# Next-to-last feed-forward chunk: two low parts of GpSimd behind VectorE's low part of B21, and the low part of B11 moved ahead of two sums

## The chip, the cores and the metric

The kernel runs on one core of one Trainium2 chip. The metric is the device time of one execution in microseconds, taken as a median over runs; the profile is one further execution with its own time.

## The reference

Two layers over a sequence of 1024 tokens with 1024 features, float32. Layer 0 mixes tokens by a gated spatial MLP, layer 1 by chunked band attention; each is followed by the same feed-forward block, which is where the change lies:

```
def swiglu(h, w_gate, w_up, w_down):
    return (jax.nn.silu(h @ w_gate) * (h @ w_up)) @ w_down

hn = rms_norm(x, norm_ffn_g[i])
x = x + swiglu(hn, ffn_w_gate[i], ffn_w_up[i], ffn_w_down[i])      # D_FF = 2816
```

## The kernel before

**Arithmetic.** Each float32 operand is split into a high part (fp32r) and a low part (the difference), and each product is three matmuls: high by high, low by high, high by low (L934 to L936). In the middle of each feed-forward block the matrix products are done in a seven-product form of a 2 by 2 blocked product. The seven left operands (weights) are called A11, A12, S2, S3, S1, A22 and S4; their right partners in the down projection are B11, B21, T2, T3, T1, T4 and B22. B parts are quarters of the hidden tensor (`h_full`, high `h_hi`, low `h_lo`, the low part written over the full one), T parts are sums of them (`t_full`, `t_hi`, `t_lo`).

**Tiling and stages.** The hidden size is cut into 11 chunks of 256. Each chunk does seven gate products, seven up products, and the seven down products of the chunk before. Chunks 2 to 8 are a loop. The next-to-last chunk ("late", number 9, `LATE`) does its own down products too, right behind its up products, with names `down_products(it, True)`; the last chunk (number 10) is written out by hand with all its gate and up products interleaved, in the order of `PROD_LAST`, and a plain down projection at its end. There are two feed-forward blocks, F1 and F2, with the same code.

**Who does what.** TensorE runs the products in a fixed order, each behind waits on semaphores: `made` (GpSimd's parts of the weights), `t_lo` (VectorE's low parts of the right side), `d_added` (VectorE's additions out of the PSUM banks). For the down products it waits in front of product number pos for `t_lo` at pos + 1, and from pos 2 on for the additions of product pos - 2 (L1103 to L1117). ScalarE makes high parts: `left_high` (L1600) of the weights, `right_high` (L1589) of the right side, in late in the order B11, B22, T1, T3, T2, then the weights at places 5 and 6, then B21 and T4. VectorE forms the hidden parts, the sums T1, T3, T2 (`first_sums`, L2084 to L2087) and T4 (`last_sum`, L2092), the low parts (`right_low`, L2078) and the additions to x (`down_adds`, L2103). GpSimd makes, group by group, the sums of weight blocks and their low parts (`middle_group`; `low` is L716, `high` is L713); the four raw weight blocks b[0] to b[3] are `raw_block`.

**Queues.** SP loads the next weight block into a `raw_block` as soon as GpSimd has finished the last low part that reads it: buffer 0 behind "lo S2", 2 behind "lo S3", 3 behind "lo A22", 1 behind "lo S4" (`gate_up`, DMA at L584). Behind the late down group, GpSimd works on the last chunk: `group` is called twice, and there it makes high parts too. It starts with the high parts of A11 (buffer 0) and A12 (buffer 1; waits for that load and for the late down product A12), then "sum S1" (L793; waits for the loads of buffers 2 and 3), then without a rest down to "lo A22". The second group is the same with the loads that the first released, except that its A12 waits for the last chunk's gate product A12; behind it come high and low parts of the last down weights (`d_hi`, `d_lo`). TensorE's down projection waits for the last of these, "lo d1".

Of the kernel before, what the change touches and what calls it, by code (L numbers as in the profile page):

```python
# [99 lines left out]
LATE = CHUNKS - 2  # L100

AT_G0, AT_D, AT_G1, AT_D_LATE = -5, -4, -3, -2
# [4 lines left out]
def middle(it, at, per, i):  # L107

    return it * (3 * per) + (at * per + i)
# [44 lines left out]
def trunk(nc, x_t, gains, v_gain, w_s_t, b_s, rel_rev, ident_d, w_units, f_blocks, f_down, out_t):  # L154
# [4 lines left out]
    with ExitStack() as ctx:  # L159
# [196 lines left out]
        def r32(ap):  # L356
            return ap.bitcast(F32)
# [84 lines left out]
        def hidden_part(t, f, h):  # L442
            return t[:, f, toks(h)]
# [4 lines left out]
        def right_full(name):  # L448
            return t_full[name][:, :] if name in t_full else hidden_part(h_full, *H_PART[name])

        def right_hi_of(name):
            return t_hi[name][:, :] if name in t_hi else hidden_part(h_hi, *H_PART[name])

        def right_lo_of(name):
            return t_lo[name][:, :] if name in t_lo else hidden_part(h_lo, *H_PART[name])
# [218 lines left out]
        def _(pool):  # L674
# [40 lines left out]
            def low(out, full, hi, made):  # L715
                pool.tensor_tensor(out, full, r32(hi), ALU.subtract).then_inc(made, 1)  # L716

            def ffn(name):
                s = hid[name]
# [21 lines left out]
                def middle_group(it, at):  # L741


                    def loaded(i):
                        pool.wait_ge(s.block_in[i], middle(it, at, 16, 16 * 4))

                    def after(op):
                        pool.wait_ge(s.made, middle(it, at, MID, MID_MADE + (MIDDLE[op] if op else 0)))

                    def low_part(op, b_, before):  # L750
                        slot = ORDER.index(op)
                        pool.wait_ge(s.left_hi, middle(it, at, 7, 7 + slot + 1))
                        after(before)
                        low(lo[slot], b_, hi[slot], s.made)

                    loaded(2)
                    loaded(3)
                    after(None)
                    pool.tensor_tensor(s1_sum[:, :], b[2], b[3], ALU.add).then_inc(s.made, 1)  # L759
                    low_part("A11", b[0], "sum S1")  # L760
                    after("lo A11")
                    pool.tensor_tensor(b[2], b[0], b[2], ALU.subtract).then_inc(s.made, 1)
                    low_part("A12", b[1], "sum S3")
                    after("lo A12")
                    pool.tensor_tensor(b[0], s1_sum[:, :], b[0], ALU.subtract).then_inc(s.made, 1)
                    after("sum S2")
                    pool.tensor_tensor(b[1], b[1], b[0], ALU.subtract).then_inc(s.made, 1)
                    low_part("S2", b[0], "sum S4")
                    low_part("S3", b[2], "lo S2")
                    low_part("S1", s1_sum[:, :], "lo S3")  # L770
                    low_part("A22", b[3], "lo S1")
                    low_part("S4", b[1], "lo A22")

# [1122 lines left out]
        def _(dve):  # L1896
# [165 lines left out]
            def ffn(name, n):  # L2062
# [9 lines left out]
                def right_low(it, name, sums=0):  # L2072

                    order = HI_LATE if isinstance(it, int) and it == LATE else HI_ORDER
                    dve.wait_ge(w.t_hi, it * 7 - 7 + (order.index(name) + 1))
                    if sums:
                        dve.wait_ge(w.t_full, it * 4 - 4 + sums)
                    dve.tensor_tensor(right_lo_of(name), right_full(name), r32(right_hi_of(name)), ALU.subtract  # L2078
                                      ).then_inc(w.t_lo, 1)

                def first_sums(it):
                    b11, b12, b22 = (hidden_part(h_full, f, h) for f, h in ((0, 0), (0, 1), (1, 1)))
                    dve.wait_ge(w.full, it * 4 + (3 if isinstance(it, int) and it == LATE else 4))
                    dve.tensor_tensor(right_full("T1"), b12, b11, ALU.subtract).then_inc(w.t_full, 1)  # L2084
                    dve.tensor_tensor(right_full("T3"), b22, b12, ALU.subtract).then_inc(w.t_full, 1)
                    dve.wait_ge(w.t_full, it * 4 - 4 + 1)
                    dve.tensor_tensor(right_full("T2"), b22, right_full("T1"), ALU.subtract).then_inc(w.t_full, 1)  # L2087
# [218 lines left out]
                def one(it, kind):  # L2306
                    if kind == "first":
                        first_chunk()
                        return
                    if kind == "last":  # L2310
                        last_chunk(it)
                        return

                    def product(g, op):
                        dve.wait_ge(w.prod, N_PROD.at(it, len(PROD) * g + PROD[op]))

                    def snap(i):
                        dve.wait_ge(w.snap, N_SNAP.at(it, i))

                    def added(i, act):  # L2320
                        dve.wait_ge(w.cadd, N_CADD.at(it, i))
                        dve.wait_ge(w.act, it * 4 + act)

                    up_order = ORDER[:5] + ["S4", "A22"] if kind == "late" else ORDER

                    def up_product(op):
                        dve.wait_ge(w.prod, N_PROD.at(it, len(PROD) + up_order.index(op) + 1))

                    if kind != "second":
                        first_sums(it - 1)  # L2330
                        last_sum(it - 1)
                        right_low(it - 1, "B11", 1)
                    if kind != "second":
                        product(0, "A12")
                        snap(1)
                        cadd(gated[0][:, :], bank[1])
                        right_low(it - 1, "B21", 4)
                        right_low(it - 1, "T2", 4)
                        right_low(it - 1, "T3")
                    product(0, "S1")  # L2340
                    snap(3)
                    cadd(gated[2][:, :], bank[0])
                    product(0, "A22")
                    cadd(gated[1][:, :], bank[1])
                    if kind != "second":
                        right_low(it - 1, "T1", 3)
                        right_low(it - 1, "T4")
                        right_low(it - 1, "B22", 3)
                        for pos in range(7):
                            down_adds(it, False, pos)  # L2350
                    up_product("A12")
                    snap(4)
                    cadd(hidden_part(h_full, 0, 0), bank[3])
                    added(4, 1)
                    times(gated[0][:, :], 0, 0)
                    up_product("S1")
                    snap(6)
                    cadd(hidden_part(h_full, 1, 1), bank[2])
                    added(5, 2)
                    times(gated[2][:, :], 1, 1)  # L2360

                    def last_01():
                        up_product("S4")
                        dve.wait_ge(w.act, it * 4 + 4)
                        dve.tensor_tensor(hidden_part(h_full, 0, 1), bank[2][:, :], gated[3][:, :], ALU.mult).then_inc(w.full, 1)

                    def last_10():
                        up_product("A22")
                        cadd(hidden_part(h_full, 1, 0), bank[3])
                        added(6, 3)  # L2370
                        times(gated[1][:, :], 1, 0)

                    if kind != "late":
                        last_10()
                        last_01()
                        return
                    last_01()
                    first_sums(it)
                    right_low(it, "B11", 1)
                    last_10()  # L2380
                    last_sum(it)
                    right_low(it, "B21", 4)
                    right_low(it, "T2", 4)
                    down_adds(it, True, 0)
                    right_low(it, "T3")
                    right_low(it, "T1", 3)
                    down_adds(it, True, 1)
                    right_low(it, "T4")
                    right_low(it, "B22", 3)
                    for pos in range(2, 7):  # L2390
                        down_adds(it, True, pos)
# [240 lines left out]
```

## Time and profile before

| what | value |
|---|---|
| median of 3 runs | 2569.73 us (2568.29 to 2572.27) |
| time of the profiled execution | 2570.11 us |
| its span | 2568.0 us, so 2.1 us lie around it |
| TensorE busy | 2448.7 us, 95% of the span |
| VectorE, ScalarE, GpSimd busy | 1679.1, 1010.8, 1286.7 us |
| mean granted clock of TensorE | 0.991 |

TensorE works nearly all the time, so a change counts by the idle time of TensorE that it adds or removes. GpSimd is busy for half of the span on average, but in the last chunk of a feed-forward block for most of the time.

### The profile page before, as it was taken

What the parts mean: (1) busy time and instruction counts of PE and PEld (TensorE: products, weight loads), DVE (VectorE), ACT (ScalarE), POOL (GpSimd) and SP (SyncE); (2) the same over time, 40 slices, a digit from 0 to 9 for tenths busy, and PEclk for the clock granted to TensorE, in tenths of its full rate; (3) what the DMA queues carried; (4) which work ended last, traced back from release to release, by engine and by line L of the source; (5) the groups of instructions that cost most, each with busy time, mean ns of one, the idle gap of its engine ahead of it and who ended that gap; (6) DMA issues with size and microseconds to landing.
All of it is one profiled execution on the core that took longest, in us unless ns stands there. A gap on an engine that the chain in (4) does not pass through costs nothing. (4 is left out here: it accounts for less than half of the span.)

```text
span 2568.0 us, 36361 instructions
## 1 busy us (share of the span) xinstructions
PE 2448.7 (95%) x11464; PEld 2019.0 (79%) x11464; DVE 1679.1 (65%) x2667; ACT 1010.8 (39%) x1831; POOL 1286.7 (50%) x898
## 2 busy tenths in 40 slices
PE   8998999999999999998989999999989999999987
PEld 7886888887788888886777777777767888888876
DVE  6246665667476777665866666676676677677755
ACT  5112211124434333331465555566544334433323
POOL 5242223213788888777312112221135878878776
PEclk9998999999999999999999999999999999999998
DMA  4232122111111211111111011111011111121111
GB/s 173 88 113 78 67 78 67 59 35 46 46 58 49 61 53 57 57 50 50 60 36 33 19 42 43 43 37 41 9 45 37 53 58 53 50 64 50 58 58 66
DMA packets 70522, 143.74 MB, mean 56 GB/s; under 512 B 7312, under 2 KB 17696, under 8 KB 69936
## 3 DMA queue, kind: packets, MB, share of 16 engines
q1 hardware_dynamic: 52912, 119.72, 14.7%
q10 hardware_dynamic: 17536, 23.07, 2.6%
q8 instruction: 42, 0.69, 0.1%
q14 instruction: 32, 0.26, 0.0%
HBM read 130.13 MB, written 12.63 MB: 56 GB/s over the span
## 5 line engine op out<-in xcount | busy, mean ns | idle before, releaser
L716 POOL TENSOR_TENSOR a_lo<-raw_block,a_hi 128x512 fp32r<-128x512 f32 x364 | 508.9, 1398 | 158.4 <-ACT a_hi L1600 134.2
L678 POOL TENSOR_SCALAR w_hi<-raw 128x1024 fp32r<-128x1024 f32 x80 | 90.7, 1133 | 830.7 <-PE bank L936 587.5
L1600 ACT ACTIVATE a_hi<-raw_block 128x512 fp32r<-128x512 f32 x324 | 202.4, 629 | 330.8 <-PE bank L936 122.4
L934 PE MATMUL bank<-T_hi,a_hi 128*128 128x512 f32 x672 | 262.6, 391 | 3.5 <-issue 3.0
L936 PE MATMUL bank<-T_hi,a_lo 128*128 128x512 f32 x672 | 261.7, 389 | 0.0
L935 PE MATMUL bank<-T_lo,a_hi 128*128 128x512 f32 x672 | 261.5, 389 | 0.0
L934 PE MATMUL bank<-B_hi,a_hi 128*128 128x512 f32 x576 | 224.9, 390 | 2.6 <-DVE h_full L2067 1.7
L936 PE MATMUL bank<-B_hi,a_lo 128*128 128x512 f32 x576 | 224.2, 389 | 0.0
L935 PE MATMUL bank<-B_lo,a_hi 128*128 128x512 f32 x576 | 224.1, 389 | 0.0
L680 POOL TENSOR_TENSOR w_lo<-raw,w_hi 128x1024 fp32r<-128x1024 f32 x80 | 198.8, 2485 | 6.7
L2067 DVE TENSOR_TENSOR h_full<-bank,h_full 128x512 f32<-128x512 f32 x54 | 37.3, 691 | 211.6 <-PE bank L936 198.2
L934 PEld LDWEIGHTS bank<-T_hi,a_hi 128*128 128x128 f32 x672 | 126.1, 188 | 33.9 <-issue 7.0
L936 PEld LDWEIGHTS bank<-T_hi,a_lo 128*128 128x128 f32 x672 | 126.1, 188 | 26.4
L935 PEld LDWEIGHTS bank<-T_lo,a_hi 128*128 128x128 f32 x672 | 126.2, 188 | 25.7
L934 PE MATMUL bank<-T_hi,w_hi 128*128 128x512 f32 x320 | 131.3, 410 | 15.6 <-issue 9.6
L2103 DVE TENSOR_TENSOR x<-bank,x 128x512 f32<-128x512 f32 x216 | 142.3, 685 | 0.0
L759 POOL TENSOR_TENSOR s_sum<-raw_block,raw_block 128x512 f32<-128x512 f32 x54 | 78.5, 1454 | 117.4 <-PE bank L936 87.6
L934 PE MATMUL bank<-B_hi,w_hi 128*128 128x512 f32 x320 | 130.0, 406 | 3.3 <-DVE B_lo L1927 1.2
L934 PEld LDWEIGHTS bank<-B_hi,a_hi 128*128 128x128 f32 x576 | 108.1, 188 | 26.5 <-POOL a_lo L716 2.5
L936 PE MATMUL bank<-T_hi,w_lo 128*128 128x512 f32 x320 | 126.6, 396 | 0.0
L935 PE MATMUL bank<-T_lo,w_hi 128*128 128x512 f32 x320 | 126.5, 395 | 0.0
L2477 DVE CUSTOM_DVE_ANT_0 prob<-scores,bias 128x640 f32<-128x640 f32 (+4 forms) x128 | 83.9, 655 | 64.6 <-PE scores L1331 33.7
(282 smaller groups left out, 6596.7 us busy)
## 6 DMA issues: line engine op xcount, KB each, us to landing
raw_block<-f_blocks_in SPq DMA_DIRECT2D x176, 256.0 KB, 2.6
raw<-w_units_in SPq DMA_DIRECT2D x80, 512.0 KB, 3.4
raw_block<-f_down_in SPq DMA_DIRECT2D x72, 256.0 KB, 3.0
v_raw<-v_scratch ACTq DMA_DIRECT2D x16, 512.0 KB, 4.1
bias<-rel_scratch ACTq DMA_DIRECT2D x8, 640.0 KB, 3.6
x<-x_t_in SPq DMA_DIRECT2D x16, 256.0 KB, 5.6
v_scratch<-atmp ACTq DMA_DIRECT2D x16, 256.0 KB, 2.4
v_scratch<-full ACTq DMA_DIRECT2D x16, 256.0 KB, 2.6
```

What stands on the lines that cost most here:

```text
L678: pool.tensor_scalar(w_hi[slot][:, :], raw[r][:, :], 1.0, 1.0, ALU.mult, ALU.mult).then_inc(w_split, 1)
L680: pool.tensor_tensor(w_lo[slot][:, :], raw[r][:, :], r32(w_hi[slot][:, :]), ALU.subtract).then_inc(w_split, 1)
L716: pool.tensor_tensor(out, full, r32(hi), ALU.subtract).then_inc(made, 1)
L759: pool.tensor_tensor(s1_sum[:, :], b[2], b[3], ALU.add).then_inc(s.made, 1)
L934: pe.matmul(out, lh, rh, start=start, stop=False, skip_group_check=read_between)
L935: pe.matmul(out, lh, rl, start=False, stop=False, skip_group_check=read_between)
L936: last = pe.matmul(out, ll, rh, start=False, stop=stop, skip_group_check=read_between)
L1600: act.activation(a_hi[pos][:, :], src[:, :], ACT.Copy).then_inc(w.left_hi, 1)
L2067: dve.tensor_tensor(dst, src[:, :], dst, ALU.add).then_inc(w.cadd, 1)
L2103: dve.tensor_tensor(x[:, k, toks(h)], bank[4 + n if op in ("A11", "S2", "S1", "S4") else n][:, :], x[:, k, toks(h)], ALU.add).then_inc(w.d ...
L2477: dve.tensor_tensor_reduce(prob[m % 3][:, off:], scores[:, SHIFT + off:SHIFT + WIN], bias[:, step(m)[1], off:], 1.0, -3.0e38, ALU.add, ALU ...
```

## The change

In `middle_group`, for the late down group alone, GpSimd waits ahead of its last two low parts (A22 and S4) until VectorE has made the second low part of the right side, B21. In VectorE's program for the late chunk, the low part of B11 moves from behind the three first sums (T1, T3, T2) to between T1 and T3.

```
                     low_part("S1", s1_sum[:, :], "lo S3")
+                    if at == AT_D_LATE:
+
+                        pool.wait_ge(s.t_lo, 7 * (LATE - 1) + 2)
                     low_part("A22", b[3], "lo S1")
                     low_part("S4", b[1], "lo A22")
...
-                def first_sums(it):
+                def first_sums(it, between=lambda: None):
                     b11, b12, b22 = (hidden_part(h_full, f, h) for f, h in ((0, 0), (0, 1), (1, 1)))
                     dve.wait_ge(w.full, it * 4 + (3 if isinstance(it, int) and it == LATE else 4))
                     dve.tensor_tensor(right_full("T1"), b12, b11, ALU.subtract).then_inc(w.t_full, 1)
+                    between()
                     dve.tensor_tensor(right_full("T3"), b22, b12, ALU.subtract).then_inc(w.t_full, 1)
...
                     last_01()
-                    first_sums(it)
-                    right_low(it, "B11", 1)
+                    first_sums(it, lambda: right_low(it, "B11", 1))
                     last_10()
```

## Rows read from the trace of the kernel before

**Rows 1.** Timeline, TensorE in F2: start, duration, engine, line, operation, idle before
```profile
2462.06 0.47 PE L934 MATMUL scores<-h_hi,a_hi 128*128 128x512 f32 x1 [0.64 <-issue]
...
2466.76 0.47 PE L934 MATMUL bank<-h_hi,a_hi 128*128 128x512 f32 x1 [1.72 <-POOL a_lo L716]
...
2487.15 0.50 PE L934 MATMUL bank<-B_hi,a_hi 128*128 128x512 f32 x1 [0.43 <-DVE x L2103]
...
2516.62 0.50 PE L934 MATMUL scores<-h_hi,d_hi 128*128 128x512 f32 x1 [1.44 <-POOL d_lo L716]
```

**Rows 2.** Timeline, TensorE in F1, the place of the last row above
```profile
1220.45 0.50 PE L934 MATMUL scores<-h_hi,d_hi 128*128 128x512 f32 x1 [1.42 <-POOL d_lo L716]
```

**Rows 3.** Timeline, VectorE in the late chunk of F2
```profile
2459.46 0.69 DVE L2084 TENSOR_TENSOR h_T_full<-h_full 128x512 f32<-128x512 f32 x1
...
2461.28 0.68 DVE L2078 TENSOR_TENSOR h_lo<-h_full,h_hi 128x512 fp32r<-128x512 f32 x1
...
2463.32 1.67 DVE L2092 TENSOR_TENSOR h_full<-h_full,h_T_full 128x512 f32<-128x512 f32 x1
2465.09 1.57 DVE L2078 TENSOR_TENSOR h_lo<-h_full,h_hi 128x512 fp32r<-128x512 f32 x1
2466.59 1.09 DVE L2078 TENSOR_TENSOR h_T_lo<-h_T_full,h_T_hi 128x512 fp32r<-128x512 f32 x1
...
2470.00 2.79 DVE L2078 TENSOR_TENSOR h_T_lo<-h_T_full,h_T_hi 128x512 fp32r<-128x512 f32 x2
2472.71 2.47 DVE L2103 TENSOR_TENSOR x<-bank,x 128x512 f32<-128x512 f32 x4
```

**Rows 4.** Timeline, ScalarE in the late chunk of F2
```profile
2460.19 1.83 ACT L1589 ACTIVATE h_T_hi<-h_T_full 128x512 fp32r<-128x512 f32 x3 [2.11 <-DVE h_T_full L2084]
2461.93 1.14 ACT L1600 ACTIVATE a_hi<-raw_block 128x512 fp32r<-128x512 f32 x2
2463.32 0.63 ACT L1589 ACTIVATE h_hi<-h_full 128x512 fp32r<-128x512 f32 x1 [0.26 <-DVE h_full L2070]
```

**Rows 5.** Timeline, GpSimd, from the late chunk into the last one, F2
```profile
2462.62 3.49 POOL L716 TENSOR_TENSOR a_lo<-raw_block,a_hi 128x512 fp32r<-128x512 f32 x2 [5.76 <-ACT a_hi L1600]
2466.09 1.05 POOL L713 TENSOR_SCALAR a_hi<-raw_block 128x512 fp32r<-128x512 f32 x1
2469.93 0.62 POOL L713 TENSOR_SCALAR a_hi<-raw_block 128x512 fp32r<-128x512 f32 x1 [2.79 <-PE bank L936]
2470.72 1.52 POOL L793 TENSOR_TENSOR s_sum<-raw_block,raw_block 128x512 f32<-128x512 f32 x1 [0.17 <-POOL a_hi L713]
...
2477.05 1.60 POOL L801 TENSOR_TENSOR raw_block<-s_sum,raw_block 128x512 f32<-128x512 f32 x1
```

**Rows 6.** Timeline, GpSimd, second group of the last chunk, F2
```profile
2493.06 0.62 POOL L713 TENSOR_SCALAR a_hi<-raw_block 128x512 fp32r<-128x512 f32 x1 [1.57 <-PE bank L936]
2493.87 1.29 POOL L793 TENSOR_TENSOR s_sum<-raw_block,raw_block 128x512 f32<-128x512 f32 x1 [0.18 <-POOL a_hi L713]
...
2514.20 2.36 POOL L716 TENSOR_TENSOR d_lo<-d_raw,d_hi 128x1024 fp32r<-128x1024 f32 x1
```

**Rows 7.** SP's DMA issues: timeline row, then median us to landing (last column)
```profile
2466.14 0.33 SPq L584 DMA_DIRECT2D raw_block<-f_blocks_in  x1
raw_block<-f_blocks_in SPq DMA_DIRECT2D x1, 256.0 KB, 2.5
...
2490.94 0.33 SPq L584 DMA_DIRECT2D raw_block<-f_blocks_in  x1
raw_block<-f_blocks_in SPq DMA_DIRECT2D x1, 256.0 KB, 2.7
```

**Rows 8.** Timeline, TensorE in F1's last down projection, behind a longer pause
```profile
1250.17 0.58 PE L934 MATMUL probs_t<-h_hi,d_hi 128*128 128x512 f32 x1 [2.28 <-DVE h_lo L2109]
```

**Rows 9.** Windows behind that pause: stretch, us, TensorE busy (count), granted clock, DMA, GB/s
```profile
1250.20:1253.60 3.40, 3.40 (x9) 0.54 0.45 154
1254.00:1257.40 3.40, 3.40 (x17) 1.00 0.40 154
```

More of the change, by code:

```diff
@@ L770, in middle_group @@
                     low_part("S1", s1_sum[:, :], "lo S3")
+                    if at == AT_D_LATE:
+                        pool.wait_ge(s.t_lo, 7 * (LATE - 1) + 2)
                     low_part("A22", b[3], "lo S1")
@@ L2079, in right_low, with first_sums @@
                                       ).then_inc(w.t_lo, 1)
-                def first_sums(it):
+                def first_sums(it, between=lambda: None):
                     b11, b12, b22 = (hidden_part(h_full, f, h) for f, h in ((0, 0), (0, 1), (1, 1)))
@@ L2084, in first_sums @@
                     dve.tensor_tensor(right_full("T1"), b12, b11, ALU.subtract).then_inc(w.t_full, 1)
+                    between()
                     dve.tensor_tensor(right_full("T3"), b22, b12, ALU.subtract).then_inc(w.t_full, 1)
@@ L2377, in one @@
                     last_01()
-                    first_sums(it)
-                    right_low(it, "B11", 1)
+                    first_sums(it, lambda: right_low(it, "B11", 1))
                     last_10()
```

## The prediction

> **What bounds the kernel now.** I read the page first: TensorE is busy for nearly the whole span, so only its pauses count. Then the list of TensorE's waits and, around the late chunk, the timeline engine by engine. In F2 TensorE pauses at these places [rows 1]: 0.64 us ahead of the down product A11 (2462.06), 1.72 ahead of A12 (2466.76), 0.43 ahead of the last chunk's first product (2487.15), and 1.44 ahead of the last down projection (2516.62). Two more stand between the second and the third, both behind VectorE's additions. F1 has the same pauses at the same distances, such as 1.42 at 1220.45 [rows 2], so every sum counts twice.
>
> The pause of 1.72 is put down to GpSimd, but the wait in the code is for several semaphores: VectorE's low part of B21 runs from 2465.09 to 2466.66, and TensorE starts 0.10 later [rows 1, 3]. The last pause, 1.44, is truly GpSimd's: its last low part of the down weights ends at 2514.20 + 2.36 = 2516.56, 0.06 before TensorE starts [rows 1, 6]. What follows in the block hangs on that moment.
>
> **What the change does, step by step (F2 times).** On VectorE the small subtractions take 0.68 to 0.69 us when alone and start 0.60 apart; those with both inputs in SBUF take longer beside GpSimd: T4's sum 1.67, B21's low part 1.57, T2's 1.09 [rows 3]. GpSimd's two low parts stand right there, from 2462.62 for 3.49 us [rows 5].
>
> *The B11 move.* T1 ends at 2460.15. The low part of B11 waits for it and starts at 2460.18 instead of 2461.28; it ends at 2460.87 instead of 2461.96 [rows 3]. The twelve matmuls of A11 fill the 2.98 us up to A12's pause, 0.47 for the first and 0.23 for each of the others [rows 1]; so with its pause of 0.64 gone and the pipeline kept full, A11 starts at about 2461.26 instead of 2462.06. T3 and T2 are each about 0.7 later, and with the two dependent starts the next VectorE operation is 0.12 later (2462.00). ScalarE made three high parts in a row from 2460.19, two of the weights after them, and was then idle 0.26 before B21's at 2463.32 [rows 4]. Now T3's high part starts at 2461.52, T2's at 2462.12, the two of the weights at 2462.64 and 2463.16, and B21's at 2463.68: 0.36 late, until 2464.31.
>
> *The GpSimd wait.* Its two low parts no longer run beside T4 and B21: T4's sum takes 0.69, from 2463.44 to 2464.13, and B21's low part waits for ScalarE, 2464.35 to 2465.03. It was 2466.66: 1.63 earlier, and TensorE's A12 comes at 2465.13. T2's low part starts behind it before GpSimd wakes, and takes 0.69. GpSimd's two low parts now run about 2465.09 to 2466.79 (held up by T2's low part, as one of 1.60 [rows 5]) and 2466.87 to 2468.16 (alone, 1.29 [rows 6]). The additions beside them read PSUM and don't take part in this.
> The trace shows it: four additions take 2.47 in all from 2472.71, with GpSimd at work all the time [rows 3, 5]. The Trainium skill, "SBUF — State Buffer", section "Who interferes with whom", says that a VectorE instruction with two SBUF inputs excludes a GpSimd one that reads SBUF, and that one with at most one SBUF input does not. By this rule each of the two meets T2's low part or nothing, and the sum stays the same.
>
> *VectorE's chain.* Between T4's start and the additions of A12, VectorE spent 1.67 + 1.57 + 1.09 + 2.79 [rows 3] on five operations that take 0.69 each when alone; Now B21's low part ends at 2465.03; from there 0.6 goes to T2, 2.4 to the four additions of A11, and 1.9 to T3 and T1 (1.2 alone, the rest for GpSimd's high part of A11, which falls between them): the additions of A12 start at about 2469.9 instead of 2472.71. TensorE is tied to this chain by its waits for additions, so it starts the last chunk about 2.9 us earlier, at 2484.2. This is all that the change gives, and it would be 5.8 us in two blocks.
>
> *What GpSimd's lateness triggers.* Queued behind the two low parts are the loads of buffers 3 and 1 and the whole of GpSimd's last chunk. "lo S4" ends at 2468.16 instead of 2466.1, so the load of buffer 1 is issued at 2468.20 instead of 2466.14 and lands 2.5 later, at 2470.70 [rows 7]. The high part of A12 ran at 2469.93, released by TensorE [rows 5]. TensorE is now early (its A12 ends at 2467.9), but the load is the last: 2470.76, **0.83 later**. From there GpSimd runs without a rest. Four of its operations, from 2470.72 to 2477.05, were stretched by VectorE to between 1.52 and 1.61 against 1.29 [rows 5, 6], 1.17 in all. In the new order T3's and T1's low parts are over by then; T4's and B22's remain, and each stretches one by 0.31: 0.62 in all. GpSimd gains 0.55 back, so its first group ends 0.83 - 0.55 = 0.28 late.
>
> *Why nothing of the 2.9 arrives.* The second group needs buffer 3, whose load is issued when the first group's last low part ends: 2490.94, landing after 2.7 at 2493.64. "sum S1" started at 2493.87, with hi A12 just ahead of it, released by TensorE at 2493.06 [rows 6, 7]. An earlier TensorE frees hi A12, but the sum can't start before the landing: at most 0.2 earlier. With the load 0.28 late it starts at about 2493.97, 0.10 late. From there to the end of "lo d1" GpSimd works with hardly a rest (22.7 us), beside the same few operations of VectorE. TensorE's lead of 2.9 turns into waits: for the second group's low part of A11 (2496.6, where TensorE would be at 2495.1), for that of S3, and for "lo d1", which comes at 2516.66 instead of 2516.56.
>
> **Sum.** Removed from TensorE's pauses in the late chunk: 2.9 per block; put back in the last chunk: 2.9 + 0.10. Net +0.1 per block, +0.2 in two. Bounds for what I haven't seen: if VectorE stretches none of GpSimd's operations, GpSimd's chain is 0.83 - 1.17 = 0.34 early (the landings move with it) and gives -0.5 per block at most; if it stretches four again, +0.83 less the 0.2 of slack at the landing gives +0.65. In two blocks -1.0 to +1.3. Against the profiled execution's 2570.11 that is 2570.3; this execution was 0.4 above the median of 2569.73, so I say 2570.0.
>
> **Rivals.**
> *A, the lead arrives.* If GpSimd's last chunk were tied to TensorE alone, or its loads came in time, all 2.9 per block would count: 2569.7 - 5.8 = 2563.9, faster by 0.23%. For it: hi A12 was released by TensorE in both groups [rows 5, 6]. Against it: 2493.64 for the landing, and "lo d1" as the last release at 2516.62. A half of it would be 2566.8.
> *B, the clock.* TensorE's pauses of the last chunk grow: about 1.7 ahead of the second group's A11, 1.9 ahead of S3, 1.7 ahead of the down projection. In F1, behind a pause of 2.28 [rows 8], the granted clock was 0.54, almost all of it at the lower level, 1.2 GHz: 9 matmuls went in 3.4 us, and 17 in the next such stretch at 1.00 [rows 9]. The eight that are missing cost 8 x 0.2 = 1.6 us. Behind the pauses of 1.44 and 1.72 the first matmul takes 0.47 or 0.50, not 0.58 [rows 1, 8], so none of this shows there. A fall behind the first two is covered by the next wait for GpSimd; one behind the pause at "lo d1" counts in full. Price: 1.6 per block, 3.2 in two, 2569.9 + 3.2 = 2573.1, or 0.13% slower; it decides if the pause passes a point between 1.72 and 2.28. It passes 0.2% only together with GpSimd's upper bound of 1.3 and a third fall.
> The Trainium skill, "TensorE: Matmul & The Clock Gate", section "HAM oscillation — how this bites in real kernels", warns of matmuls that turn cold behind long pauses; by it the bigger pauses here could lower the clock, at the price just worked out. The 2.28 pause agrees.
> *C, the change does not do what it says.* B21's low part is as late as before, because ScalarE's B21 high part is queued behind T3, T2 and two weights. I find it 0.36 late only, with 1.63 to spare; it would need 1.6 more. Then nothing gained and GpSimd late by up to 2: +1 per block, 2571.9.
>
> **How the numbers follow.** Forecast 0.68, A 0.12 (the full and the half alike), B 0.12, C 0.08. A run of this kernel differs by up to 2.5 us from the median, and 0.2% is 5.1 us, about what a measurement can tell from no change. The forecast, B and C stay inside; only A in full goes below, half of its chance and a little for effects that I have not seen: faster 0.07; B with everything against it: slower 0.04; same 0.89. Range: from A's half, 2566.5, to B's 2573.1.
>
> **What would show it.** In the changed profile: B11's low part before T3, starting 0.7 behind T1; T4's sum and B21's low part 0.69 each; A12's matmul on TensorE about 1.6 earlier; GpSimd's two low parts behind B21's; the load of buffer 1 2.0 later and hi A12 0.8 later, released by a DMA; TensorE at the last chunk 2.9 earlier; then pauses for GpSimd of 1.5 or more at three places, and "lo d1" within 0.7 of its old time relative to the late chunk's start. I am wrong if the second group's "sum S1" starts over 0.5 earlier, or if the granted clock falls behind "lo d1".

## The result: 0.15% slower, and the profile after

The changed kernel takes 2575.2 us (median of 18 runs, 2567.59 to 2579.33), the kernel before 2571.25 us beside it (18 runs, 2566.82 to 2574.61). The ratio is 1.0015, 95% interval 1.0009 to 1.0022. The prediction was 2570.0 us and "no change", range 2566.5 to 2573.1. Of the 5.2 us that are missing, 1.5 are the starting point (2569.73 from three runs, 2571.25 from eighteen); the loss itself is 3.9 us, where I had 0.2. The profiled execution of the changed kernel has a span of 2569.4 us against 2568.0. That difference is not the loss: in this pair of traces the ends of the two feed-forward blocks are 2.8 us longer in sum (table below), while the rest happens to be 1.5 us shorter.

I read the late chunk and the last chunk again, by engine. Below, a "block" is one feed-forward block, F1 or F2. TensorE in F2, timeline as in [rows 1] (lines are three to four higher in the changed file):

```profile
2464.99 0.47 PE L937 MATMUL bank<-h_hi,a_hi 128*128 128x512 f32 x1 [1.07 <-issue]
2475.98 0.47 PE L937 MATMUL scores<-h_T_hi,a_hi 128*128 128x512 f32 x1 [2.52 <-DVE x L2107]
2484.86 0.50 PE L937 MATMUL bank<-B_hi,a_hi 128*128 128x512 f32 x1 [0.45 <-DVE x L2107]
2498.56 0.50 PE L937 MATMUL bank<-B_hi,a_hi 128*128 128x512 f32 x1 [2.49 <-POOL a_lo L716]
2518.63 0.50 PE L937 MATMUL scores<-h_hi,d_hi 128*128 128x512 f32 x1 [1.50 <-POOL d_lo L716]
```

VectorE in the late chunk, as [rows 3]:

```profile
2459.25 0.69 DVE L2087 TENSOR_TENSOR h_T_full<-h_full 128x512 f32<-128x512 f32 x1
2460.05 0.69 DVE L2081 TENSOR_TENSOR h_lo<-h_full,h_hi 128x512 fp32r<-128x512 f32 x1
...
2463.30 0.69 DVE L2096 TENSOR_TENSOR h_full<-h_full,h_T_full 128x512 f32<-128x512 f32 x1
2464.20 0.69 DVE L2081 TENSOR_TENSOR h_lo<-h_full,h_hi 128x512 fp32r<-128x512 f32 x1 [0.21 <-ACT h_hi L1592]
2464.81 0.68 DVE L2081 TENSOR_TENSOR h_T_lo<-h_T_full,h_T_hi 128x512 fp32r<-128x512 f32 x1
```

The whole chunk stands 0.21 us earlier in this trace (T1's sum at 2459.25, not 2459.46), so later times are best read from T1's sum. TensorE's A12 is 1.56 earlier than before by that measure, its last chunk 2.08 earlier (25.61 us behind T1's sum, not 27.69). And then it pauses 2.49 us for the second group's low part of A11, and starts the down projection 59.38 us behind T1's sum, not 57.16: **2.2 us late**. In F1 it is 0.6 late (1219.06 - 1161.30 = 57.76, against 57.15).

GpSimd in F2 [rows 5, 6]:

```profile
2464.97 3.11 POOL L716 TENSOR_TENSOR a_lo<-raw_block,a_hi 128x512 fp32r<-128x512 f32 x2 [8.30 <-DVE h_lo L2081]
...
2470.93 0.62 POOL L713 TENSOR_SCALAR a_hi<-raw_block 128x512 fp32r<-128x512 f32 x1 [1.82 <-PE probs_t L939]
2471.73 1.29 POOL L796 TENSOR_TENSOR s_sum<-raw_block,raw_block 128x512 f32<-128x512 f32 x1 [0.17 <-POOL a_hi L713]
...
2492.94 0.62 POOL L713 TENSOR_SCALAR a_hi<-raw_block 128x512 fp32r<-128x512 f32 x1 [0.96 <-DMA raw_block<-f_blocks_in]
2495.91 1.26 POOL L796 TENSOR_TENSOR s_sum<-raw_block,raw_block 128x512 f32<-128x512 f32 x1 [2.35 <-DMA raw_block<-f_blocks_in]
...
2516.22 2.36 POOL L716 TENSOR_TENSOR d_lo<-d_raw,d_hi 128x1024 fp32r<-128x1024 f32 x1
```

and in F1:

```profile
1173.03 0.62 POOL L713 TENSOR_SCALAR a_hi<-raw_block 128x512 fp32r<-128x512 f32 x1 [1.86 <-DMA raw_block<-f_blocks_in]
...
1196.41 1.29 POOL L796 TENSOR_TENSOR s_sum<-raw_block,raw_block 128x512 f32<-128x512 f32 x1 [0.82 <-DMA raw_block<-f_blocks_in]
```

The two blocks are alike up to the second group. Its sum S1 waits for a DMA in both, for 0.82 us in F1 and for 2.35 us in F2. That load is buffer 3's. The DMA view of the stretch from its issue to its landing (queue: packets, MB, share; then the issues with median us to landing), F2:

```profile
q1 hardware_dynamic: 372, 1.36, 88.6%
q8 instruction: 1, 0.02, 1.9%
issues: line engine op xcount, KB each, median us to landing
d_raw<-f_down_in SPq DMA_DIRECT2D x1, 1024.0 KB, 6.3
raw_block<-f_blocks_in SPq DMA_DIRECT2D x1, 256.0 KB, 4.4
```

and F1, where no row of q8 stands:

```profile
q1 hardware_dynamic: 304, 0.75, 76.2%
issues: line engine op xcount, KB each, median us to landing
d_raw<-f_down_in SPq DMA_DIRECT2D x1, 1024.0 KB, 6.3
raw_block<-f_blocks_in SPq DMA_DIRECT2D x1, 256.0 KB, 2.8
```

In F2 one 16 KB packet of q8, a queue that the profile marks "instruction", falls into the load, and the load takes 4.4 us; in F1 none does, and it takes 2.8. Before, it took 2.7 [rows 7]. I call such a packet a fetch. The 1 MB load is there in both.

### The profile page after: what moved, and what is told of

Same layout as the page of the kernel before. It is cut to its first block and busy times, and to the rows that moved or that the text cites. A ratio compares the mean times of both kernels' runs of the same rounds, so it can differ in the third digit from the quotient of the medians.

```text
span 2569.4 us, 36361 instructions
## 1 busy us (share of the span) xinstructions
PE 2449.2 (95%) x11464; PEld 2020.2 (79%) x11464; DVE 1674.4 (65%) x2667; ACT 1010.7 (39%) x1831; POOL 1285.2 (50%) x898
## 5 line engine op out<-in xcount | busy, mean ns | idle before, releaser
L939 PEld LDWEIGHTS bank<-B_hi,a_lo 128*128 128x128 f32 x576 | 108.4, 188 | 22.8
L938 PEld LDWEIGHTS bank<-B_lo,a_hi 128*128 128x128 f32 x576 | 108.6, 189 | 22.4
```

The costliest lines, as they stand in the source:

```text
L938: pe.matmul(out, lh, rl, start=False, stop=False, skip_group_check=read_between)
L939: last = pe.matmul(out, ll, rh, start=False, stop=stop, skip_group_check=read_between)
```

## The experiments

**Theories.** L: GpSimd's last chunk sets the end of each block, and the change starts it late because buffers 3 and 1 are released late. F: TensorE's lead, not used for anything, brings a fetch forward into the load of buffer 3. F was put up after the first traces; the expectations name it from "TensorE's lead taken away" on. Rivals: K, VectorE's and ScalarE's new order costs the time; C, the granted clock falls in the longer pauses.

All comparisons are with the kernel before, run beside the experiment on the same chip. "End" is the time from the start of T1's sum to the end of GpSimd's last low part, F1 and F2; "buffer 3" is the time from issue to landing of the second group's load of buffer 3, with a star where a packet of q8 falls into it.

| kernel | ratio (95%) | end, us | buffer 3, us |
|---|---|---|---|
| before | | 57.10, 57.10 | 2.6, 2.7 |
| changed | 1.0015 (1.0009 to 1.0022) | 57.71, 59.32 | 2.8, 4.4* |
| a2_changed_again | 1.0011 (1.0002 to 1.0020) | 57.44, 59.05 | 2.6, 4.0* |
| a3_changed | 1.0015 (1.0006 to 1.0025) | 59.67, 57.51 | 5.0*, 2.6 |
| e1_b11_only | 1.0011 (1.0001 to 1.0021) | 57.33, 57.33 | 2.7, 2.4 |
| e2_wait_only | 1.0009 (1.0000 to 1.0018) | 56.91, 56.86 | 2.4, 2.5 |
| e3_wait_t3 | 1.0034 (1.0021 to 1.0047) | 60.57, 61.62 | 2.7, 2.5 |
| e4_late_loads | 1.0020 (1.0009 to 1.0031) | 58.63, 57.48 | 2.8, 2.6 |
| e5_after_late_draw | 1.0013 (1.0004 to 1.0022) | 59.25, 59.53 | 4.5*, 3.9* |
| e7_swap | 1.0007 (0.9998 to 1.0016) | 58.94, 57.56 | 4.7*, 3.6* |
| e8_after_act_dhi | 1.0008 (0.9999 to 1.0017) | 57.42, 57.61 | 4.6*, 4.8* |
| e9_before_act_dhi | 1.0006 (0.9996 to 1.0015) | 54.95, 54.89 | 2.8, 2.6 |
| e10_hold | 1.0012 (1.0003 to 1.0021) | 57.52, 58.12 | 2.8, 2.8 |
| r10_hold | 1.0002 (0.9993 to 1.0011) | 57.50, 57.73 | 2.6, 2.6 |
| e11_swap_hold | 0.9998 (0.9989 to 1.0007) | 56.91, 57.36 | 2.8, 2.5 |
| e12_wait_swap_hold | 0.9998 (0.9988 to 1.0007) | 57.09, 56.89 | 2.9, 2.8 |
| r12_wait_swap_hold | 0.9996 (0.9987 to 1.0005) | 57.26, 57.11 | 2.7, 2.8 |
| n1_before_again | 1.0001 (0.9992 to 1.0010) | 57.65, 57.15 | 3.3, 2.8 |

(In the two ScalarE versions, e8 and e9, the down projection doesn't hang on that end alone.)

**One part at a time.** The changed kernel without GpSimd's wait:

```
-                        pool.wait_ge(s.t_lo, 7 * (LATE - 1) + 2)
```

> The B11 move alone, without GpSimd's wait. Theory L (the loss comes from GpSimd's last-chunk chain, which starts late because the loads of buffers 3 and 1 are released late): GpSimd's two low parts stay where they were, the load of buffer 1 is issued as early as before, so the time stays within 0.1% of the kernel before (ratio 0.999 to 1.001). B11's low part on VectorE ends 1.1 us earlier. Rival K (the reordered VectorE and ScalarE work, with B21's high part 0.36 us later, costs the time): 1.0015, as the changed kernel.

1.0011; the block ends are 0.23 late, not more. TensorE's pause ahead of A12 grew instead:

```profile
2467.72 0.47 PE L934 MATMUL bank<-h_hi,a_hi 128*128 128x512 f32 x1 [2.88 <-POOL a_lo L716]
```

With B21's low part no earlier, what the B11 move gives at A11 comes back as pause at A12 (2.88, was 1.72 [rows 1]). The measured ratio is above the 0.999 to 1.001 that I expected of L; its interval holds both answers.

The wait alone, B11 at its old place:

> GpSimd's wait alone, B11's low part at its old place. Theory L: the loads are released at about 2466.6 and 2468.1 (F2, relative to a late chunk at its old place) as in the changed kernel, so the time is that of the changed kernel, 1.0015 of the kernel before (1.0008 to 1.0022). Rival K: no change, 1.000.

1.0009, while this trace has both ends 0.2 *early*, although both loads are issued about 2 us late: the clock fell in the down products of both blocks here, and no fetch met the load. So late loads do not make a late end in every case. Neither run decides between L and K by its time.

**Dose.** GpSimd waits for the fourth low part:

```
-                        pool.wait_ge(s.t_lo, 7 * (LATE - 1) + 2)
+                        pool.wait_ge(s.t_lo, 7 * (LATE - 1) + 4)
```

> The changed kernel with GpSimd waiting for the fourth low part of the right side (T3) instead of the second (B21), about 3.5 us later. Theory L: a dose test; both loads and GpSimd's last chunk go 3.5 us later still, there is no slack left in either feed-forward block, so about 3.5 us per block, 7 in all, on top of the changed kernel: 1.0035 to 1.0045 of the kernel before. Rival K, and a rival C (the loss is a fall of TensorE's granted clock that comes with the longer pauses, whatever their length): no more than the changed kernel's 1.0015.

1.0034, a little under the expected 1.0035 to 1.0045, and ends 3.5 and 4.5 us late; TensorE's pause for the second group's A11 is 5.84 us in F1:

```profile
1201.58 0.79 PE L937 MATMUL bank<-B_hi,a_hi 128*128 128x512 f32 x1 [5.84 <-POOL a_lo L716]
```

L held, K fell, and so did C in the form that it has above. GpSimd's two low parts and both loads are 3.6 us later than in the changed kernel. The ends are 2.9 to 4.2 us later than in those three of its blocks that have no fetch in the load (57.4 to 57.7); here the fetch comes at 31.3 and 31.5 us behind T1's sum, ahead of the load of buffer 3 at 35.1. So the delay goes through nearly one for one. In time the five runs show 4.9 us more than the changed kernel, not the 7 that I expected, with an interval of 3.3 us to either side.

**The loads alone.** SP waits, nobody else:

```
+                    if op == "lo A22":
+                        sp.wait_ge(s.t_lo, 7 * (LATE - 1) + 2)
+                    if op == "lo S4":
+                        sp.wait_ge(s.d_added, D_SUMS * (LATE - 1) + 1)
```

> The kernel before, where only SP waits: the load of buffer 3 for B21's low part, that of buffer 1 for the first addition of the late down products (about 2466.7 and 2468.3 on F2's old times instead of 2464.5 and 2466.1). GpSimd, VectorE, ScalarE and TensorE have their old order. Theory L: the load of buffer 1 lands at about 2471, hi A12 is about 1 us late and with it the rest of the last chunk: 1 us or more per block, ratio 1.0008 to 1.002. If the loads are not the cause but GpSimd's own late work or TensorE's early arrival: 1.000.

1.0020, ends 1.5 and 0.4 late. Here late loads alone make the kernel slower. In F1 hi A12 was 2.1 late, because the first group's load of buffer 1 took 3.5 us with a packet of q8 in it; in F2 it was 1.0 late with 2.35 us for that load. That pointed to fetches.

**The changed kernel again.**

> The changed kernel once more, for a second profile and times beside the next three. Theory L (late loads): from VectorE's T1 sum to the start of the last down projection 57.5 to 59.5 us in each block (57.15 before; 57.8 and 59.4 in the first profile), and in the second group GpSimd's A12 and sum S1 released by DMAs again. Rival C (clock): that stretch is as before within 0.3 us and the loss is in more stretches at the lower clock elsewhere. Ratio 1.0015 by both.

1.0011, the same picture: F2 with the fetch and 4.0 us, F1 without. The ends are 0.3 and 1.95 us late, so C in the form "that stretch is as before within 0.3 us" fell for F2.

**The 1 MB load out of the way.**

```
+                sp.wait_ge(s.made, MADE_LAST + LAST["sum S1"])
                 d_units(CHUNKS - 1)
```

> The changed kernel with the 1 MB load of the last down weights issued behind the second group's sum S1 instead of 0.4 us behind the load of buffer 3. Theory L with a crowded landing: buffer 3 lands in 2.5 us instead of 2.8 and 4.4, so 0.3 to 1.9 us per block are given back, ratio to the kernel before 1.0005 or less. If the 4.4 came from something else (an instruction fetch in the same stretch), or if the clock is the cause: 1.0012 to 1.0015, as the changed kernel.

1.0013, no gain. Buffer 3 in F1, its own stretch:

```profile
q1 hardware_dynamic: 274, 0.50, 36.5%
q8 instruction: 1, 0.02, 1.8%
issues: line engine op xcount, KB each, median us to landing
raw_block<-f_blocks_in SPq DMA_DIRECT2D x1, 256.0 KB, 4.5
```

4.5 us with the queue otherwise at 36.5% instead of 88.6%: the 1 MB load is not the cause, the fetch is there again. That was the other answer in the expectation, and the ratio lies in its band.

**The two low parts exchanged.** S4 first, so buffer 1 is released first; TensorE's and SP's waits follow.

```
+                    if at == AT_D_LATE:
+                        low_part("S4", b[1], "lo S1")
+                        low_part("A22", b[3], "lo A22")
+                        return
```

> The changed kernel with GpSimd's last two low parts of the late down group exchanged, S4 first, so that buffer 1 is released 1.4 us earlier and buffer 3 1.4 us later. Theory L: hi A12 no longer waits for buffer 1, sum S1 of the first group waits for buffer 3 and starts 0.5 to 0.8 us earlier than in the changed kernel; the gain carries to the end of the block: 1.0 to 1.6 us less in all than the changed kernel. Rival C: no difference.

1.0007, 2.7 us less than the changed kernel beside it, with intervals that overlap. Sum S1 of the first group starts 0.7 to 0.9 earlier than in the changed kernel, as expected, but both loads of buffer 3 met a fetch and the gain shows only in part.

**ScalarE for the last high parts.**

```
+                    act.wait_ge(w.d_in, 32)
+                    for f in range(2):
+                        act.activation(d_hi[:, f, :], d_raw[:, f, :], ACT.Copy).then_inc(w.d_hi, 1)
```

> The changed kernel with the two high parts of the last down weights made by ScalarE, which is idle there, instead of GpSimd. Theory L: GpSimd's chain to the last low part loses 2 x 1.2 us and TensorE's pause ahead of the down projection, 1.3 to 1.5 us, nearly goes: about 1.3 us less per block, 2.6 in all, than the changed kernel, ratio to the kernel before 1.0005 or less. Rival C: no more than 1 us less.

> The kernel before, with the two high parts of the last down weights made by ScalarE. In the changed kernel the same step took away TensorE's pause for GpSimd but gave a new one of 1.6 us for VectorE's second low part of the hidden tensor. Expected here: the pause ahead of the down projection falls from 1.4 us to nearly nothing and 1.0 to 1.6 us come back 2.7 us later; 0 to 0.4 us gained per block, ratio 0.9997 to 1.0001.

1.0008 and 1.0006. In e9, the kernel before with this step, GpSimd's end comes 2.2 earlier, and TensorE has another wait one step on:

```profile
2519.66 0.50 PE L940 MATMUL scores<-h_hi,d_hi 128*128 128x512 f32 x1 [1.60 <-DVE h_lo L2118]
```

My 2.6 us for e8 failed. e9's reading of the waits was right, though its ratio lies above the expected 1.0001 (interval from 0.9996): VectorE's second low part of the hidden tensor is nearly as late as GpSimd was. So a block's end hangs on GpSimd's last low part only as long as GpSimd is not early.

**TensorE's lead taken away.** TensorE waits ahead of the last chunk:

```
                     pe.wait_ge(s.d_added, D_SUMS * (LATE - 1) + (4 * 5 + 4))
+                    pe.wait_ge(s.made, MADE_LAST + MADE["hi S4"])
```

> The changed kernel, where TensorE waits ahead of the last chunk's first product until GpSimd has made the high part of S4 in its first group, so that TensorE starts that chunk about 27.3 us after VectorE's T1 sum, as in the kernel before (27.7), not at 25.6. Theory F (TensorE's lead brings an instruction fetch forward into the landing of buffer 3, which costs 1.5 to 2 us whenever no fall of the clock has taken the lead away): the fetch comes at 35 us or later, buffer 3 lands in 2.5 to 2.9 us, sum S1 of the second group starts at 34.7 to 35.2 in both blocks, and the ratio to the kernel before falls to 1.0003 to 1.0006. If the long landings have nothing to do with TensorE's lead, one of the two blocks still shows 36 us or more and the ratio stays at 1.001 or above, or rises because a pause was added.

> The changed kernel with TensorE's hold, a second time: fetch at 36 us or later and buffer 3 landed in 2.9 us or less in both blocks, ends at 57.5 to 58.2; 1 to 2.5 us less than the changed kernel beside it.

1.0012 and 1.0002. In all four blocks the fetch comes after the landing, and the load takes 2.6 to 2.8. The second trace in F2:

```profile
q1 hardware_dynamic: 303, 0.75, 88.8%
issues: line engine op xcount, KB each, median us to landing
d_raw<-f_down_in SPq DMA_DIRECT2D x1, 1024.0 KB, 5.3
raw_block<-f_blocks_in SPq DMA_DIRECT2D x1, 256.0 KB, 2.6
```

No fall of the clock is near the down products or the hold in these four blocks, so the hold alone did it. A wait added to TensorE makes the blocks end earlier: 1.0 to 1.5 us late in two blocks together, against 2.3 to 3.0 in the three traces of the changed kernel. The times do not show it beyond the noise: the second ratio is lower (2573.27 us beside 2575.72 for the changed kernel, but the intervals overlap), and the first, 1.0012, lies where I had put the rival answer.

> The changed kernel a third time. Theory F: in each block either the clock has fallen in the down products and the fetch comes after 35.5 us (block end at 57.4 to 57.8), or it has not, the fetch comes at 33 to 34 us, buffer 3 takes 3.9 us or more to land, and the block ends at 59.0 to 59.4. Ratio 1.001 to 1.0015.

1.0015, and the roles of the blocks are reversed: F1 collides, F2 doesn't. That is what theory F had said ahead of the run, with an end of 59.67 in F1 where I had at most 59.4. F1's load:

```profile
q8 instruction: 1, 0.02, 2.2%
raw_block<-f_blocks_in SPq DMA_DIRECT2D x1, 256.0 KB, 5.0
```

What differs is the granted clock in the down products (two stretches: length, TensorE busy, clock, DMA, GB/s), F1 and F2:

```profile
1179.30:1182.70 3.40, 3.40 (x16) 1.00 0.00 0
2478.30:2481.70 3.40, 2.67 (x6) 0.53 0.00 0
```

Where it falls to 0.53, at 1.2 GHz but for its edges, TensorE loses about 1.6 us there by estimate (3.4 x 0.47), of which 1.0 is left at the last chunk: it starts that chunk 26.32 us behind T1's sum in F2 and 25.29 in F1. The fetch comes at 35.8 us in F2, behind the landing, and at 33.6 in F1. That holds in all six blocks of the three traces of the changed kernel: three falls in the down products, and those three blocks alone are free of the fetch in the load.

The start of TensorE's last chunk sorts the blocks of all 18 traces. In e3 it is 23.62 us behind T1's sum, and the fetch passes ahead of the late load. In the other 34 blocks, all nine that start at 24.7 to 25.8 us have the fetch in the load of buffer 3, and none of the 25 that start at 26.1 or later. But the fetch does not simply follow that start: in the changed kernel it comes 7.8 to 8.3 us behind it where it collides and 9.4 to 10.1 where it doesn't. What sets its time exactly stays open.

**The parts together.**

> The exchanged low parts (S4 ahead of A22) and TensorE's hold together. Theory F: no collision, and GpSimd's first group 0.7 us earlier than in the changed kernel; sum S1 of the second group at 34.1 to 34.6 us after the T1 sum in both blocks (34.4 before), ratio 0.9998 to 1.0003. Otherwise as for the hold alone.

> GpSimd's wait without the B11 move, with the exchange and the hold. The wait alone had sum S1 at 34.3 us in both blocks; with the exchange 33.8 to 34.3, so up to 0.5 us per block under the kernel before: ratio 0.9995 to 1.0002. It is the version with the best chance to be no slower than the kernel before.

> GpSimd's wait, the exchange and the hold, without the B11 move, a second time: block ends at 56.9 to 57.1 as before, ratio to the kernel before 0.9993 to 1.0003, and 2 to 3.5 us less than the changed kernel beside it.

0.9998, 0.9998 and 0.9996: the loss is gone. Wait, exchange and hold without the B11 move are level with the kernel before and do not beat it beyond the interval; r12 stood 4.8 us under the changed kernel beside it (2570.94 and 2575.72), and these two intervals don't overlap. In five of the six blocks of these three traces the clock also fell right behind the hold or in the down products, so TensorE's lead was taken away twice there; the clean test of the hold is the one above.

**No change at all.**

> The kernel before, unchanged, timed as if it were a changed one. If the comparison has no offset: ratio within 0.9993 to 1.0007 and 57.1 us from the T1 sum to the end of GpSimd's last low part in both blocks. If every run kernel comes out 1.5 to 2.5 us over its reference for reasons outside the blocks: 1.0006 to 1.001.

1.0001: two sets of runs of one kernel agree. One block of this trace has 3.3 us for buffer 3 without a fetch and ends 0.55 late, so a fetch is not the only thing that stretches a load.

## Why the prediction was wrong, step by step

- *The B11 move and the wait in the late chunk*: right. B11's low part 0.80 behind T1, T4's sum and B21's low part 0.69 each, B21's high part late by a few tenths, TensorE's A12 1.56 earlier (1.63 said), both GpSimd parts behind B21's.
- *VectorE's chain*: additions of A12 at 2469.57 (2469.9 said), but T4's and B22's low parts then took 3.27 instead of 2.42 beside GpSimd, so TensorE's lead at the last chunk is 2.1 in F2, not 2.9 (1.0 in F1, where the clock fell in the down products). The size was off, without consequence for the sum, since none of the lead arrives.
- *GpSimd's lateness*: the mechanism was right. hi A12 was 1.2 late in the first trace, not 0.83: the load was issued 0.1 later than I had it, landed in 2.65 instead of 2.5, and GpSimd starts up to 0.2 behind a landing. With 0.5 given back, the first group ends 0.7 late instead of the 0.28 I said: buffer 3 is issued 32.20 and 32.17 us behind T1's sum, and 31.47 before. That is behind the 0.3 to 0.6 us of the blocks without a fetch in the load, where I said 0.10.
- *The step that failed*: "landing after 2.7", in the paragraph on why nothing of the 2.9 arrives. I carried the landing of the second group's buffer 3 over unchanged from one trace and put it in no bound; an earlier TensorE was taken to change nothing there. In the changed kernel's three traces it took 4.4, 4.0 and 5.0 us in three of six blocks, and such a block ends 1.95 to 2.6 late, not 0.1. The sum per execution is then (0.61 + 2.22), (0.34 + 1.95) and (2.57 + 0.41): 2.8, 2.3 and 3.0 us, 0.09% to 0.12%. I had 0.2 with an upper bound of 1.3. The blocks without the fetch alone would have stayed inside that bound (0.3 to 0.6 each).
- *Rival A* (the lead arrives) did not come. *Rival C* neither. *Rival B*: the clock does fall more often, but in other places than the one with a price: in the down products or behind the pause for the second group's A11 (2.2 to 3.2 us), once in each of the six blocks, where the next wait for GpSimd covers it, and never behind "lo d1" in these traces. The length of the pause alone doesn't decide, as I had it: in the changed kernel's down products the clock fell at pauses of 2.50, 2.52 and 2.60 us and did not at 2.20, 2.52 and 2.60. The Trainium skill's warning, "TensorE: Matmul & The Clock Gate", section "HAM oscillation — how this bites in real kernels", is of waits of 3 to 5 us in its example; the traces agree that TensorE runs at half clock behind some pauses (0.53 above), but show it behind shorter ones, and not each time.
- *A slip in the range*: A's half is 2566.8, and the range begins at 2566.5. Nothing hangs on it.

**How far this is shown.** The stretched load and the fetch: in 18 traces of 36 blocks (the table's), the second group's load of buffer 3 took 3.6 to 5.0 us in 9 of 9 cases with a packet of q8 in it, and 2.4 to 2.9 in 26 of 27 without. Of all 216 block loads that are issued from T1's sum to the end of these blocks, a packet of q8 starts during 33, and 31 of those took 2.96 us or more (the other two 2.6 and 2.7); of the 183 others, 4 took that long, and in three of the four such a packet had started just before the issue. Moving the 1 MB load away changed nothing, moving TensorE back freed all four blocks. That the fetch is TensorE's is inferred from its moving with TensorE. It is not tied to GpSimd or SP: in e3 both were 3.6 us later, and the fetch came earlier. ScalarE and VectorE, which wait for TensorE there, are not excluded.

The measured losses of the changed kernel (2.8 to 3.9 us) are matched by the traces' 2.3 to 3.0 within their intervals. A smaller cause beside it is not excluded: the mean granted clock of the changed kernel's runs was lower too (0.9898 and 0.9886 in the second and third set, against 0.9914 and 0.9906 of the kernel before beside them). One fall like the one shown is 0.0006 of the mean (1.6 of 2570), so this is about three more of them per execution, by estimate; one per block is covered, as said, and one more elsewhere would cost up to 1.6 us. Open stays why the B11 move alone and the wait alone measured 1.0011 and 1.0009 with ends 0.2 late and early: their intervals reach to 1.0001 and 1.0000, and they had 11 runs each. Their mean clock was also lower (0.9900 and 0.9894 against 0.9908).

## What to carry to other kernels

Before you let an engine run ahead, follow the engine that it then waits for: a lead that is given back at the next wait is worth nothing, and it can move what the leading engine triggers, here most likely a transfer of its code, into another engine's load. A load that lands with 0.2 us to spare belongs in the sum with a range, not with the duration of one trace. And delaying an engine delays every buffer that it releases: here two low parts 2 us later meant two loads 2 us later, most of that was absorbed by slack (0.3 to 0.6 us were left at the end), and with the slack used up 3.6 us more cost 2.9 to 4.2 per block.

## What the runs showed of the hardware

A 256 KB load that lands in 2.3 to 2.9 us took up to 5.0 us when one 16 KB packet of the instruction queue q8 fell into it, also with the 1 MB load moved away (4.5 us). The 8 KB packets of the second instruction queue, q14, did not do that: 14 of the block loads had one in them and none of q8, and they took 2.3 to 2.8 us (one in e9's F1, 2.8). And the blocks of the changed kernel in which the granted clock fell to 0.53 in the down products ended 1.6 to 2.2 us *earlier* than the others of their trace (57.71 and 59.32, 57.44 and 59.05, 57.51 and 59.67): the packet then came after the load.
